# Two heads' probabilities transposed into one PSUM bank and copied by one ScalarE pass, in the first 48 heads of each layer

## Chip, cores and metric

The kernel runs on one core of a Trainium2 chip. The metric is the device time of one execution in microseconds, as the median of the runs. Engines are written PE (TensorE), DVE (VectorE), ACT (ScalarE), POOL (GpSimd) and SP (SyncE); QB, below, is the projection of the second head group's queries.

## What is computed

A decoder trunk of two layers over 512 positions and a width of 1024, in fp32. Each layer has a mixer with two groups of eight heads of 64 (group A: a sliding window of 128 with a sink for each head; group B: the 128 keys with the highest indexer score for each query), then a SwiGLU of width 2816. Cut to the part that the change touches:

```python
# group A, blocks of 128 queries against the previous and the own block of keys
s = einsum('bnqhgd,bnkhd->bnhgqk', qb, kk) * D ** -0.5      # masked to the band
p = softmax(concat([s, sink], -1), axis=-1)[..., :-1]
o = einsum('bnhgqk,bnkhd->bnqhgd', p, vv)
# group B, 128 queries against the selected keys (here: all keys up to the block, the others masked)
p = softmax(where(valid, s, -inf), axis=-1)
o = einsum('bqhgn,bqnhd->bqhgd', p, vs)
y = concat([rms_norm(ya, g_a), rms_norm(yb, g_b)], -1) @ w_o
```

## The kernel before

It is written engine by engine, in raw queues: each engine runs a fixed list of instructions in order, and semaphores (`wait_ge`) tie the lists together. Weights stream in as pieces of 128x1024; ACT rounds a piece to a high half, DVE (or POOL) subtracts it to get the low half, and PE forms each product from three matmuls (`split_product`, L631 to L633).

Attention of a layer is one software pipeline, `attention(l)`, which stands on PE (L1047), on ACT (L1398) and on DVE (L1926) with the same step counter i. It goes over 64 heads n = 8u + h: eight units u of eight heads. Units 0 to 3 are group A, tiles 0 to 3 of 128 queries; units 4 to 7 are group B, tiles 0, 1, 3, 2. A head has as many key blocks of 128 as `keys_of` says: 1 in unit 0, 2 in units 1 to 3, 1 in unit 4, 2 in unit 5, 4 in unit 6, 3 in unit 7. So the first 48 heads have at most 256 keys.

In step i, in this order:

- PE: scores of head i (`head_scores`, L941; from head 48 on two heads at a time every second step, `pair_scores`), transposes of the probabilities of head i-3 (`transpose_p`, L962), in the steps of `QB_STEPS` (1, 4, 6, 9, 11, 14, 16, 19, 21, 24, 26, 29, 31) a projection step of six matmuls of 512 columns (`project_qb`), values of head i-5 (`head_values`, L974), in steps 9, 21, 30 and 45 the transposes of roped queries (`transpose_q`), and every eighth step the transposes of a finished y (`transpose_y`).
- ACT: the copy of the transposed probabilities of head i-3 from PSUM to `pT` (`copy_p`, L1365; in units 6 and 7 heads 3 and 7 are copied by DVE instead, L1743), the exponential of head i (`exponential`, L1357), after some steps the evacuation of a projection, the square, scaling and high half of a finished y, a copy of transposed queries, and in steps 42, 47, 52 and 57 a weight conversion.
- DVE: rounds of the top-128 search (`top_max`, `top_replace`), the mask of head i (`mask_scores`, L1719), which writes `prob`, and the normalisation and low half of a finished y.

Scores lie in banks 3 and 4 in turn (three banks from head 40 on), so the score of head n waits for the mask of head n-2. The transposed probabilities lie in bank 6 or 7 by the parity of the head, so the transposes of head n wait for the copy of head n-2 (`wait_pT`, L380). `prob` and `pT` are rings of four slots of 512 columns; the mask of head n waits for the transposes of head n-4, the copy of head n for the values of head n-4. With L970 the page means the transposes, with L992 the value products, with L959 and L938 the scores, with L1371 ACT's copy, with L1362 its exponential, with L1739 the mask.

Of the kernel before, what the change touches and what calls it, by code (L numbers as in the profile page):

```python
# [11 lines left out]
ACT = mybir.ActivationFunctionType  # L12
# [53 lines left out]
PAIRS_FROM = 48  # L66
PT_RING = 4
# [49 lines left out]
def build_trunk(nc, x, c_col, positions, inv_freq, weights, w_ada, b_ada, b_gate, ln_col, ln_row, sinks, g_col, out):  # L117
    with ExitStack() as ctx:
# [260 lines left out]

        def wait_pT(eng, l, u, h):  # L380

            flat = [(a, b) for a in range(8) for b in range(HEADS) if (a, b) <= (u, h)]
            n_dve = sum(on_dve(a, b) for a, b in flat)
            if on_dve(u, h):
                eng.wait_ge(pT_dve, l * dve_heads + n_dve)
            else:
                eng.wait_ge(pT_act, l * (64 - dve_heads) + len(flat) - n_dve)
# [234 lines left out]
        def _(pe):  # L622
# [339 lines left out]
            def transpose_p(l, u, h):  # L962
                lo, hi = keys_of(UNITS[u])
                pe.wait_ge(probs, at_head(l, u, h))
                if before := back(u, h, 2):

                    wait_pT(pe, l, *before)
                n = 8 * u + h
                for b in range((hi - lo) // P):
                    m = pe.transpose(bank[6 + h % 2][:, b * P:(b + 1) * P],  # L970
                                     prob[:, n % P_RING, b * P:(b + 1) * P], ident[:])
                m.then_inc(p_transposed, 1)

            def head_values(l, u, h):  # L974
# [16 lines left out]
                for b in range(nb):  # L991
                    m = pe.matmul(bank[u % 2][:, h * HD:h * HD + w], pT[:, h % PT_RING, b * P:(b + 1) * P],  # L992
# [54 lines left out]
            def attention(l):  # L1047
                in_bank2 = ("chunk", 3)
                for i in range(64 + LAG_Y):
# [4 lines left out]
                    if 0 <= i - LAG_T < 64:  # L1054
                        transpose_p(l, (i - LAG_T) // 8, (i - LAG_T) % 8)
# [211 lines left out]
        def _(act):  # L1267
# [89 lines left out]
            def exponential(l, u, h):  # L1357
# [3 lines left out]
                p = prob[:, n % P_RING, 0:hi - lo]  # L1361
# [3 lines left out]
            def copy_p(l, u, h):  # L1365
                lo, hi = keys_of(UNITS[u])
                act.wait_ge(p_transposed, at_head(l, u, h))
                if before := back(u, h, PT_RING):

                    act.wait_ge(av_done, at_head(l, *before))  # L1370
                nc.scalar.activation(pT[:, h % PT_RING, 0:hi - lo], bank[6 + h % 2][:, 0:hi - lo], ACT.Copy)\  # L1371
# [26 lines left out]
            def attention(l):  # L1398
                for i in range(64 + LAG_SPLIT):
                    if 0 <= i - LAG_T < 64:  # L1400
                        u, h = (i - LAG_T) // 8, (i - LAG_T) % 8
                        if not on_dve(u, h):
# [122 lines left out]
        def _(dve):  # L1525
# [193 lines left out]
            def mask_scores(l, u, h):  # L1719
# [6 lines left out]
                if n >= P_RING:  # L1726
                    dve.wait_ge(p_transposed, at_head(l, u, h) - P_RING)
# [11 lines left out]
                nc.vector.tensor_tensor_reduce(out=prob[:, n % P_RING, 0:hi - lo], in0=s_bank(n)[:, 0:hi - lo],  # L1739
# [460 lines left out]
```

## Time and profile before

| | |
|---|---|
| median of 3 runs | 1275.48 us (1275.37 to 1276.41) |
| the profiled execution | 1276.25 us, of which the span is 1274.6 us |
| granted clock of TensorE | 0.998 of full speed |
| busy: PE, DVE, ACT, POOL | 1235.8, 801.5, 510.5, 274.2 us |
| attention loops | about 128 to 236 us (layer 0) and 751 to 855 us (layer 1) |

The profile is one execution of the program. Its tables give busy time by engine, groups of instructions by source line and shape, with the idle time of the engine just ahead of them and what ended that idle time (the releaser), and timelines: one row for each instruction or run of equal instructions, by its start in us from the start of the span. A matmul row's duration reaches beyond the start of the next one, because matmuls are pipelined; the distance between starts is their pitch. The same holds in part for ACT and DVE. PE is busy nearly all the time, so what is read in the timelines is where it is not, and how far ahead of its reader each ACT or DVE result comes.

### The profile page before, as it was taken

What the parts mean: (1) busy time and instruction counts of PE and PEld (TensorE: products, weight loads), DVE (VectorE), ACT (ScalarE), POOL (GpSimd) and SP (SyncE); (2) the same over time, 40 slices, a digit from 0 to 9 for tenths busy, and PEclk for the clock granted to TensorE, in tenths of its full rate; (3) what the DMA queues carried; (4) which work ended last, traced back from release to release, by engine and by line L of the source; (5) the groups of instructions that cost most, each with busy time, mean ns of one, the idle gap of its engine ahead of it and who ended that gap; (6) DMA issues with size and microseconds to landing.
All of it is one profiled execution on the core that took longest, in us unless ns stands there. A gap on an engine that the chain in (4) does not pass through costs nothing. (4 is left out here: it accounts for less than half of the span.)

```text
span 1274.6 us, 18347 instructions
## 1 busy us (share of the span) xinstructions
PE 1235.8 (97%) x6394; PEld 1031.6 (81%) x6394; DVE 801.5 (63%) x1400; ACT 510.5 (40%) x1027; POOL 274.2 (22%) x281
## 2 busy tenths in 40 slices
PE   6999989999999999999999999999999999999997
PEld 5778876889888888888888688778988888888886
DVE  6889997677777764333676699856733355433338
ACT  3555568345232212222145466862643321222220
POOL 4027236600111010000007367570000000000000
PEclk9999999999999999999999999999999999999999
DMA  9672012334878554222523120112232223332211
GB/s 358 240 270 79 33 51 67 132 116 150 279 264 270 193 168 175 90 93 98 171 94 117 66 67 2 37 63 84 75 124 99 97 101 132 99 98 89 94 65 66
DMA packets 44850, 158.30 MB, mean 124 GB/s; under 512 B 5872, under 2 KB 5872, under 8 KB 44784
## 3 DMA queue, kind: packets, MB, share of 16 engines
q1 hardware_dynamic: 30528, 109.07, 24.8%
q0 software_dynamic: 12960, 47.19, 10.9%
q10 hardware_dynamic: 1296, 1.17, 0.3%
q8 instruction: 40, 0.66, 0.2%
q14 instruction: 26, 0.21, 0.1%
HBM read 155.31 MB, written 2.10 MB: 123 GB/s over the span
## 5 line engine op out<-in xcount | busy, mean ns | idle before, releaser
L631 PE MATMUL bank<-hT_hi,w_hi 128*128 128x512 f32 x640 | 249.5, 390 | 0.0
L633 PE MATMUL bank<-hT_hi,w_lo 128*128 128x512 f32 x640 | 249.0, 389 | 0.0
L632 PE MATMUL bank<-hT_lo,w_hi 128*128 128x512 f32 x640 | 249.0, 389 | 0.0
L1967 DVE TENSOR_TENSOR w_lo<-w_raw,w_hi 128x1024 fp32r<-128x1024 f32 x88 | 107.9, 1226 | 147.0 <-ACT w_hi L1434 147.0
L1280 ACT ACTIVATE w_hi<-w_raw 128x1024 fp32r<-128x1024 f32 x96 | 100.7, 1062 | 202.8 <-PE bank L633 189.0
L1434 ACT ACTIVATE w_hi<-w_raw 128x1024 fp32r<-128x1024 f32 x88 | 93.0, 1057 | 161.1 <-PE bank L633 155.8
L631 PE MATMUL bank<-w_hi,hT_hi 128*128 128x512 f32 (+2 forms) x392 | 148.1, 378 | 2.9 <-ACT pq L1316 2.0
L1544 DVE TENSOR_TENSOR w_lo<-w_raw,w_hi 128x1024 fp32r<-128x1024 f32 x88 | 114.1, 1310 | 53.6 <-ACT w_hi L1280 52.2
L633 PE MATMUL bank<-w_hi,hT_lo 128*128 128x512 f32 (+2 forms) x392 | 142.6, 364 | 0.0
L632 PE MATMUL bank<-w_lo,hT_hi 128*128 128x512 f32 (+2 forms) x392 | 142.3, 363 | 0.0
L633 PEld LDWEIGHTS bank<-hT_hi,w_lo 128*128 128x128 f32 x640 | 120.1, 188 | 25.3
L631 PEld LDWEIGHTS bank<-hT_hi,w_hi 128*128 128x128 f32 x640 | 120.1, 188 | 24.8
L632 PEld LDWEIGHTS bank<-hT_lo,w_hi 128*128 128x128 f32 x640 | 120.1, 188 | 24.6
L631 PE MATMUL bank<-w_hi,gu_hi 128*128 128x512 f32 x264 | 102.9, 390 | 0.0
L633 PE MATMUL bank<-w_hi,gu_lo 128*128 128x512 f32 x264 | 102.7, 389 | 0.0
L632 PE MATMUL bank<-w_lo,gu_hi 128*128 128x512 f32 x264 | 102.7, 389 | 0.0
L478 POOL TENSOR_TENSOR rs_out<-rs_in,minus_half 128x1 f32<-128x1 f32 x31 | 21.4, 690 | 349.8 <-DVE rs_in L1814 325.3
L1993 DVE TENSOR_TENSOR gu<-bank,silu_g 128x512 f32<-128x512 f32 x44 | 30.4, 692 | 102.2 <-PE bank L633 101.8
L631 PEld LDWEIGHTS bank<-w_hi,hT_hi 128*128 128x128 f32 x392 | 73.9, 188 | 21.6 <-issue 7.0
L1427 ACT ACTIVATE silu_g<-bank 128x512 f32<-128x512 f32 x44 | 26.3, 598 | 156.2 <-PE bank L633 149.7
L633 PEld LDWEIGHTS bank<-w_hi,hT_lo 128*128 128x128 f32 x392 | 73.8, 188 | 11.6
L632 PEld LDWEIGHTS bank<-w_lo,hT_hi 128*128 128x128 f32 x392 | 74.0, 189 | 9.9 <-issue 0.5
(207 smaller groups left out, 2199.5 us busy)
## 6 DMA issues: line engine op xcount, KB each, us to landing
w_raw<-in_weights SPq DMA_DIRECT2D x184, 512.0 KB, 3.5
ada_w<-in_w_ada POOLq DMA_DIRECT2D x80, 512.0 KB, 5.2
ada_w<-in_w_ada SPq DMA_DIRECT2D x4, 512.0 KB, 6.6
qT<-in_w_ada SPq DMA_DIRECT2D x4, 512.0 KB, 10.0
xs<-in_x SPq DMA_DIRECT2D x4, 512.0 KB, 15.4
g_row<-in_ln_row POOLq DMA_DIRECT2D x4, 512.0 KB, 5.2
b_row<-in_ln_row POOLq DMA_DIRECT2D x4, 512.0 KB, 6.1
trunk_out<-xs SPq DMA_DIRECT2D x8, 256.0 KB, 2.1
```

The lines of the kernel that those rows point to most:

```text
L478: nc.gpsimd.tensor_tensor(rs_out[:, n:n + 1], rs_in[:, n:n + 1], minus_half[:], ALU.pow)\
L631: pe.matmul(dst, a_hi, b_hi, start=first, stop=False)
L632: pe.matmul(dst, a_hi, b_lo, start=False, stop=False)
L633: return pe.matmul(dst, a_lo, b_hi, start=False, stop=last)
L1280: nc.scalar.activation(w_hi[:, p % RING, :], w_raw[:, p % RING, :], ACT.Copy).then_inc(hi_ready, 1)
L1427: nc.scalar.activation(silu_g[:, f, :], bank[GU_BANK[g] + 2 * f][:], ACT.Silu)\
L1434: nc.scalar.activation(w_hi[:, s, :], w_raw[:, s, :], ACT.Copy).then_inc(hi_ready, 1)
L1544: nc.vector.tensor_tensor(w_lo[:, p % RING, :], w_raw[:, p % RING, :], w_hi[:, p % RING, :].bitcast(F32), ALU.subtract).then_inc(lo_ready, 1)
L1967: nc.vector.tensor_tensor(w_lo[:, s, :], w_raw[:, s, :], w_hi[:, s, :].bitcast(F32), ALU.subtract).then_inc(lo_ready, 1)
L1993: nc.vector.tensor_tensor(gu[:, f, :], bank[GU_BANK[g] + 2 * f + 1][:], silu_g[:, f, :], ALU.mult).then_inc(gu_ready, 1)
```

## The change

For heads n below `NARROW` = 48, the heads are handled in pairs (n even, n+1). PE does the transposes of both in the step in which it did those of the odd one (step n+4), into one bank: the even head's blocks in the first half of the used columns, the odd one's behind; pairs alternate between banks 6 and 7. ACT copies the pair by one pass of up to 512 columns into one slot of `pT`, at the place where it copied the odd head; the copy of the even head is gone. `prob` holds eight heads, two in a slot of 512 columns, and the mask of head n waits for the transposes of head n-8. The value products read their half of the slot and wait for the pair's copy. The copy waits for the values of eight heads before (the slot's last user). From head 48 on the code is as before, with its semaphore counts adjusted.

```diff
--- before.py
+++ after.py
@@ -64,6 +64,7 @@
 
 QB_FREE = 40
 PAIRS_FROM = 48
+NARROW = 48
 PT_RING = 4
 DVE_HEADS = (3, 7)
 
@@ -377,14 +378,29 @@
 
         dve_heads = 2 * len(DVE_HEADS)
 
+        def prob_of(n, w):
+
+            if n < NARROW:
+                return prob[:, n % 8 // 2, n % 2 * 256:n % 2 * 256 + w]
+            return prob[:, n % P_RING, 0:w]
+
+        def pT_of(n, w):
+
+            if n < NARROW:
+                return pT[:, n // 2 % PT_RING, n % 2 * w:(n % 2 + 1) * w]
+            return pT[:, n % PT_RING, 0:w]
+
         def wait_pT(eng, l, u, h):
 
-            flat = [(a, b) for a in range(8) for b in range(HEADS) if (a, b) <= (u, h)]
-            n_dve = sum(on_dve(a, b) for a, b in flat)
+            n = 8 * u + h
+            n_dve = sum(on_dve(m // HEADS, m % HEADS) for m in range(n + 1))
+            by_act = NARROW // 2 + 64 - NARROW - dve_heads
             if on_dve(u, h):
                 eng.wait_ge(pT_dve, l * dve_heads + n_dve)
+            elif n < NARROW:
+                eng.wait_ge(pT_act, l * by_act + n // 2 + 1)
             else:
-                eng.wait_ge(pT_act, l * (64 - dve_heads) + len(flat) - n_dve)
+                eng.wait_ge(pT_act, l * by_act + n + 1 - NARROW // 2 - n_dve)
 
         def back(u, h, n):
 
@@ -961,14 +977,19 @@
 
             def transpose_p(l, u, h):
                 lo, hi = keys_of(UNITS[u])
+                n = 8 * u + h
+                w = hi - lo
                 pe.wait_ge(probs, at_head(l, u, h))
-                if before := back(u, h, 2):
+                if before := back(u, h, 2 if n >= NARROW else 3 + h % 2):
 
                     wait_pT(pe, l, *before)
-                n = 8 * u + h
-                for b in range((hi - lo) // P):
-                    m = pe.transpose(bank[6 + h % 2][:, b * P:(b + 1) * P],
-                                     prob[:, n % P_RING, b * P:(b + 1) * P], ident[:])
+                if n < NARROW:
+                    b0, at = 6 + n // 2 % 2, n % 2 * w
+                else:
+                    b0, at = 6 + h % 2, 0
+                for b in range(w // P):
+                    m = pe.transpose(bank[b0][:, at + b * P:at + (b + 1) * P],
+                                     prob_of(n, w)[:, b * P:(b + 1) * P], ident[:])
                 m.then_inc(p_transposed, 1)
 
             def head_values(l, u, h):
@@ -989,7 +1010,8 @@
 
                 w = P if h < HEADS - 1 else HD
                 for b in range(nb):
-                    m = pe.matmul(bank[u % 2][:, h * HD:h * HD + w], pT[:, h % PT_RING, b * P:(b + 1) * P],
+                    m = pe.matmul(bank[u % 2][:, h * HD:h * HD + w],
+                                  pT_of(8 * u + h, hi - lo)[:, b * P:(b + 1) * P],
                                   v[:, lo // P + b, g:g + w], start=b == 0, stop=b == nb - 1)
                 m.then_inc(av_done, 1)
 
@@ -1051,7 +1073,10 @@
                         head_scores(l, i // 8, i % 8)
                     elif i < 64 and i % 2 == 0:
                         pair_scores(l, i // 8, i % 8)
-                    if 0 <= i - LAG_T < 64:
+                    if 0 <= i - LAG_T < NARROW and (i - LAG_T) % 2 == 1:
+                        transpose_p(l, (i - LAG_T - 1) // 8, (i - LAG_T - 1) % 8)
+                        transpose_p(l, (i - LAG_T) // 8, (i - LAG_T) % 8)
+                    elif NARROW <= i - LAG_T < 64:
                         transpose_p(l, (i - LAG_T) // 8, (i - LAG_T) % 8)
                     if i in QB_STEPS:
                         project_qb(l, QB_STEPS.index(i) // CP[4], QB_STEPS.index(i) % CP[4])
@@ -1358,16 +1383,21 @@
                 lo, hi = keys_of(UNITS[u])
                 n = 8 * u + h
                 act.wait_ge(masked, at_head(l, u, h))
-                p = prob[:, n % P_RING, 0:hi - lo]
+                p = prob_of(n, hi - lo)
                 nc.scalar.activation(p, p, ACT.Exp, scale=-1.0, bias=nmax[:, u % 2, h:h + 1],
                                      accum_out=rowsum[:, u % 2, h:h + 1]).then_inc(probs, 1)
 
             def copy_p(l, u, h):
                 lo, hi = keys_of(UNITS[u])
+                n = 8 * u + h
                 act.wait_ge(p_transposed, at_head(l, u, h))
-                if before := back(u, h, PT_RING):
+                if before := back(u, h, 8 if n < NARROW else PT_RING):
 
                     act.wait_ge(av_done, at_head(l, *before))
+                if n < NARROW:
+                    nc.scalar.activation(pT[:, n // 2 % PT_RING, 0:2 * (hi - lo)],
+                                         bank[6 + n // 2 % 2][:, 0:2 * (hi - lo)], ACT.Copy).then_inc(pT_act, 1)
+                    return
                 nc.scalar.activation(pT[:, h % PT_RING, 0:hi - lo], bank[6 + h % 2][:, 0:hi - lo], ACT.Copy)\
                     .then_inc(pT_act, 1)
 
@@ -1399,7 +1429,7 @@
                 for i in range(64 + LAG_SPLIT):
                     if 0 <= i - LAG_T < 64:
                         u, h = (i - LAG_T) // 8, (i - LAG_T) % 8
-                        if not on_dve(u, h):
+                        if not on_dve(u, h) and (i - LAG_T >= NARROW or h % 2 == 1):
                             copy_p(l, u, h)
                     if i < 64:
                         exponential(l, i // 8, i % 8)
@@ -1723,8 +1753,9 @@
                 n = 8 * u + h
                 dve.wait_ge(scored, at_head(l, u, h))
 
-                if n >= P_RING:
-                    dve.wait_ge(p_transposed, at_head(l, u, h) - P_RING)
+                ring = 2 * P_RING if n < NARROW else P_RING
+                if n >= ring:
+                    dve.wait_ge(p_transposed, at_head(l, u, h) - ring)
                 else:
                     dve.wait_ge(qk_transposed, at_chunk(l, 2, T - 1))
                 if h == 0 and u >= 2:
@@ -1736,7 +1767,7 @@
                 else:
                     mask = scores[:, SC_AT[t]:SC_AT[t] + hi - lo] if t > 0 else band[:, P:2 * P]
                     start = 3.0e38
-                nc.vector.tensor_tensor_reduce(out=prob[:, n % P_RING, 0:hi - lo], in0=s_bank(n)[:, 0:hi - lo],
+                nc.vector.tensor_tensor_reduce(out=prob_of(n, hi - lo), in0=s_bank(n)[:, 0:hi - lo],
                                                in1=mask, scale=-(HD ** -0.5), scalar=start, op0=ALU.add,
                                                op1=ALU.min, accum_out=nmax[:, u % 2, h:h + 1]).then_inc(masked, 1)
```

## Rows read from the trace of the kernel before

**Rows 1.** The page, part 1: busy us, share of the span, instructions.

```profile
PE 1235.8 (97%) x6394; PEld 1031.6 (81%) x6394; DVE 801.5 (63%) x1400; ACT 510.5 (40%) x1027; POOL 274.2 (22%) x281
```

**Rows 2.** Windows of the attention loops: us, busy us (x instructions) by engine, clock, DMA.

```profile
core 0: us, PE busy (x) PEld busy (x) DVE busy (x) ACT busy (x) POOL busy (x), PEclk, DMA share, GB/s
...
140.00:183.00 43.00, 41.40 (x255) 35.10 (x254) 41.85 (x132) 26.85 (x86) 11.37 (x12) 1.00 0.11 38
183.00:200.00 17.00, 12.82 (x90) 10.71 (x91) 12.55 (x53) 13.30 (x49) 11.36 (x10) 1.00 0.20 63
200.00:212.00 12.00, 11.80 (x84) 8.73 (x82) 9.30 (x32) 10.73 (x31) 9.25 (x7) 1.00 0.27 89
212.00:240.00 28.00, 26.85 (x192) 21.80 (x193) 16.91 (x43) 19.50 (x47) 21.84 (x15) 1.00 0.13 39
750.00:860.00 110.00, 103.96 (x687) 86.47 (x686) 85.97 (x294) 77.30 (x238) 75.51 (x59) 1.00 0.10 34
```

**Rows 3.** Groups by shape: count, busy us, mean ns, idle before and its releaser.

```profile
L970 PE MATMUL bank<-ident,pq 128*128 128x128 f32 x272 | 51.8, 277 | 6.2 <-ACT pT L1371 5.1 <-DVE pT L1749 1.1
...
L1371 ACT ACTIVATE pT<-bank 128x256 f32<-128x256 f32 x64 | 23.9, 373 | 5.1 <-PE bank L970 5.1
...
L1371 ACT ACTIVATE pT<-bank 128x512 f32<-128x512 f32 x12 | 7.0, 585 | 0.0
```

**Rows 4.** Timeline of PE, layer 0: start, us, instruction [idle before <-releaser].

```profile
164.12 0.61 PE L992 MATMUL bank<-v_a,pT 128*128 128x128 f32 x4
165.13 0.70 PE L959 MATMUL bank<-kT,qT 128*128 128x256 f32 x2 [0.40 <-DVE nmax L1739]
166.01 0.41 PE L970 MATMUL bank<-ident,pq 128*128 128x128 f32 x2 [0.18 <-ACT pT L1371]
166.89 0.50 PE L631 MATMUL bank<-w_hi,hT_hi 128*128 128x512 f32 x1 [0.47 <-ACT pq L1316]
...
181.79 0.38 PE L970 MATMUL bank<-ident,pq 128*128 128x128 f32 x2
...
183.47 0.38 PE L970 MATMUL bank<-ident,pq 128*128 128x128 f32 x2
183.69 0.61 PE L992 MATMUL bank<-v_a,pT 128*128 128x128 f32 x4
...
185.27 0.41 PE L970 MATMUL bank<-ident,pq 128*128 128x128 f32 x2 [0.75 <-ACT pT L1371]
```

**Rows 5.** Timeline of ACT, layer 0, copies of heads 19 and 29.

```profile
165.49 0.38 ACT L1371 ACTIVATE pT<-bank 128x256 f32<-128x256 f32 x1
...
184.76 0.36 ACT L1371 ACTIVATE pT<-bank 128x256 f32<-128x256 f32 x1
```

**Rows 6.** Timeline of PE, layer 0: q transposes, values of heads 42 and 44.

```profile
199.76 0.63 PE L898 MATMUL bank<-ident,pq 128*128 128x128 f32 x4 [0.84 <-DVE hT_lo L1789]
...
201.97 0.61 PE L992 MATMUL bank<-v_b,pT 128*128 128x128 f32 x4
...
204.58 0.61 PE L992 MATMUL bank<-v_b,pT 128*128 128x128 f32 x4
```

**Rows 7.** Timeline of ACT, layer 0: copy 43, exponential 46, copy 45.

```profile
202.34 0.37 ACT L1371 ACTIVATE pT<-bank 128x256 f32<-128x256 f32 x1
202.60 0.51 ACT L1362 ACTIVATE pq<-pq,nmax 128x256 f32<-128x256 f32 x1
...
205.41 0.38 ACT L1371 ACTIVATE pT<-bank 128x256 f32<-128x256 f32 x1
```

**Rows 8.** Timeline of PE, layer 1: values 18, a projection step, values 28.

```profile
786.02 0.61 PE L992 MATMUL bank<-v_a,pT 128*128 128x128 f32 x4
...
787.77 0.50 PE L631 MATMUL bank<-w_hi,hT_hi 128*128 128x512 f32 x1 [0.47 <-ACT pq L1316]
...
803.77 0.61 PE L992 MATMUL bank<-v_a,pT 128*128 128x128 f32 x4
```

**Rows 9.** Timeline of ACT, layer 1, copies of heads 19 and 29.

```profile
786.37 0.37 ACT L1371 ACTIVATE pT<-bank 128x256 f32<-128x256 f32 x1
...
803.63 0.36 ACT L1371 ACTIVATE pT<-bank 128x256 f32<-128x256 f32 x1
```

## The prediction, made before the changed kernel ran

> **What bounds the kernel now.** I read the busy times of the page first, then the table by stretch, the groups by shape, and last the timelines of TensorE (PE) and ScalarE (ACT), step by step. PE is busy 97% of the span [rows 1], so only its idle time can be won or lost. No matmul or transpose is added or removed; the forecast is therefore a sum of PE waits inside the two attention loops. In layer 0's loop PE idles 1.6 of 43 us while VectorE (DVE) is 97% busy (140 to 183 us), then 4.2 of 17, 0.2 of 12 and 1.15 of 28 us; ACT is busy 62%, 78% and 89% of the first three stretches. Layer 1 idles 6.0 of 110 us [rows 2]. After the loop PE has no idle time worth the name until the next stage, so a microsecond that PE loses in the loop is lost at the end.
>
> **How a head's copy stands to its readers.** Call T(n) the transposes of head n, C(n) its copy, A(n) its value product. PE does T(n) in step n+3 and A(n) in step n+5; ACT does C(n) in step n+3, behind the exponential of head n+2. The change makes T(n), T(n+1) of an even head and their one copy all happen in step n+4. Three things follow for A(n), n even:
> - By the end of T(n+1) PE has done the same work as before, so that moment stays. A(n) comes one T earlier, because T(n+2) is no longer in between: a T of two blocks has a pitch of 0.22 us (183.47 to 183.69) [rows 4].
> - The pair's copy can start no earlier than C(n+1) does today, since ACT still does the exponential of n+3 first. It takes 0.59 us instead of 0.37, by the form of 512 columns [rows 3]. I use 0.60, plus 0.04 for the hand-over to PE.
> - So A(n) is late by (start of C(n+1) + 0.64) - (start of A(n) - 0.22). Today A(n) needs only C(n), which is one ACT step older.
>
> Where a projection step (six 512-column matmuls) or a y transpose lies between T(n+1) and A(n), the wait is hidden by it: so it is, step by step in the timelines, for heads 0 to 6, 14, 16 and 20 to 26. Without that cover, A(n) follows T(n+1) by only 0.88 us (one A and one score), and ACT, which does two exponentials, a root's scaling or a 1 us conversion in front, is later than that.
>
> **The sum, layer 0.** Waits don't add up: a PE that has waited once comes later to the next place, so each place counts against the shift that is there already, and today's waits behind it vanish.
> - Head 18: C(19) starts at 165.49, A(18) at 164.12 [rows 5, 4]: 166.13 - 163.90 = 2.2 us late. Behind it three waits vanish (0.40, 0.18, 0.47) [rows 4]: 1.2 us stay. Heads 8, 10 and 12 are late too, by less; they lie ahead of it and are contained in it.
> - Head 28: C(29) at 184.76, A(28) at 183.69: 185.40 - 183.47 = 1.9 late [rows 4, 5]; the 0.75 wait at 185.27 vanishes [rows 4]: 1.2. But C(29) is itself behind DVE, which is full until 183 and which the first shift of 1.2 sets back (a full queue that is started later ends later), by an estimated 0.2. I take 1.4 us; ends 0.7 (DVE catches up) and 1.9 (the 0.75 isn't recovered).
> - Heads 34 to 40: late as well, but at 199.76 PE waits 0.84 for DVE's low half of y [rows 6], which hangs on ACT; ACT gets there no later with one copy fewer. Nothing is added: that wait is the cover. Were it gone, this would cost another 0.8.
> - Head 42: C(43) starts at 202.34 [rows 7]; its ACT step then holds one copy fewer, so about 202.1, done 202.7; A(42) would come at 201.9 [rows 6]: 0.8 late. Head 44: C(45) at 205.41, behind a scaling and a conversion, about 205.2 in the new order, so A(44) at 205.8 in place of 204.58 [rows 6, 7]; with T(46) (0.22) still to be done and matmul tails of 0.1 taken off, 1.4 us. No QB step, y transpose or DVE wait stands there. Ends 0.8 (ACT gains more) and 1.7 (A(44) waits for the full ACT order of today).
> - Heads 48 to 63 keep their code. All idle time there is 1.15 us [rows 2], part of it waits on DVE that move with PE. I give back 0.35; ends 0 and 1.15.
>
> Layer 0: 1.4 + 0 + 1.4 - 0.35 = 2.45 us.
>
> **Layer 1.** Head 18: C(19) at 786.37, A(18) at 786.02 [rows 8, 9]: 787.01 - 785.80 = 1.2 late, less the 0.47 wait at 787.77 [rows 8]: 0.7. Head 28: C(29) at 803.63, A(28) at 803.77: 804.27 - 803.55 = 0.7 late [rows 8, 9] against unshifted queues; DVE is nearly full here too and mostly moves with the shift, so I add about two thirds: 1.2; ends 0.7 and 1.5. The rest is the same pattern to 0.1 us. 1.2 + 1.4 - 0.35 = 2.25 us.
>
> **What comes free.** 24 ACT copies a layer fall away, but the next ACT instruction starts 0.26 us after a copy of 256 columns (202.34 to 202.60) [rows 7] and, by my estimate from the duration of the 512 form, about 0.48 after one of 512: 0.04 a pair, 1.9 us in all of ACT, off PE's path except where used above. PE's waits for a free transpose bank (5.1 us in all, heads behind 48 included) [rows 3] vanish in the first 48 heads; the sum has them, since each was set against the wait that takes its place. Probabilities in eight slots in place of four: DVE masks head n behind its score, and T(n-4) stands ahead of that score in PE's queue today, so that wait is never the last and lifting it is worth 0; eight slots are needed only because T of an even head now comes behind the score of head n+4. At the border, T(48) waits for the copy of heads 46 and 47: PE first does one A and the y transposes, 0.44 us each by the pitch of such groups, and the copy needs 0.64: 0 to 0.5, taken 0. No DMA is moved; POOL's root and gain work follows ACT's conversions and moves with them.
>
> ACT is not saturated outside 200 to 212 us, and its lateness is what PE waits for [rows 2]. The Trainium skill (Perfetto Trace Analysis, Optimizing Scalar/DVE Operations) says that grouping into larger operations helps if the engine is saturated, and that where Scalar or Vector are not saturated but cause bubbles elsewhere, breaking instructions up may let work finish sooner. By the first sentence the change would win, by the second lose; this trace's 62% and 78% stand on the second's side. By the first alone the sum would be a gain of the 1.9 us of ACT, 1273.6 us; by the second it is the sum below.
>
> **Sum.** 2.45 + 2.25 = 4.7 us. The profiled execution took 1276.25 us (span 1274.6 and 1.65 around it), so 1280.95 for it; that execution is 0.77 above the median of the three runs (1275.48), so **1280.2 us** for the median.
>
> **Rivals.**
> - *The early shift is absorbed.* ACT and DVE have enough lead that heads 18 and 28 cost nothing net, and only heads 42 to 44 do: 2 x 1.05 = 2.1 us, 1277.6 us. For it: DVE, not PE, limits 140 to 183 [rows 2], and PE waited for it at 165.13 [rows 4]. Against: A(28) lies behind that, and its own copy is late. Chance 0.21.
> - *Faster: the bank waits were the limit.* One mechanism: PE's waits for a transpose bank vanish (up to 5.1 us) [rows 3] and A(n) finds its copy done, because ACT's order has room. It decides if the pair's copy ends within 0.88 us of T(n+1), that is, if ACT idles when T(n+1) ends. Price -3 to -5: about 1271.6 us. For it: those waits are real [rows 4]. Against: ACT doesn't idle there: C(29) starts 2.6 us behind the end of T(29) (181.79 + 0.38 to 184.76) [rows 4, 5]. Chance 0.08.
> - *The waits add up.* The shift is passed on by DVE and ACT to every later copy, so that the late heads, thirteen a layer, all count. The six priced above run from 0.7 to 2.2 us; at an estimated 1 us each they make 26, less the bank waits 21. Half of that is about 11 us: 1287 us. Against: the cover at 199.76 [rows 6]. Chance 0.08.
> - The forecast itself: 0.63.
>
> **Chances.** A measurement of this kernel tells about 0.2% (2.6 us) from no change. Slower by more: 0.63 less a tenth for its low end, plus 0.08, plus a quarter of the first rival: 0.70. Within: 0.20. Faster: 0.10. The ends of the terms give +2.0 to +7 us (1277.5 to 1282.5); the range reaches down through the first rival, 1276.0, and up halfway to the third, 1284.5.
>
> **What would show it.** Right: PE idle ahead of the value products (L992's line) that is absent now, at heads 10, 12, 18, 28, 34, 36 and 40 to 44, ended by ACT's copy; copies of 512 columns at 0.59 us; idle ahead of the transposes nearly gone in the first 48 heads; PE busy unchanged. A(44) of layer 0 about 2.8 us later than 204.58. Wrong: copies that start within 0.2 us of T(n+1); new waits at the score products or in DVE that are longer than the old ones; a shift at 200 us of zero.

## The result, and the profile after

The changed kernel takes 1280.87 us (median of 6 runs, 1279.41 to 1282.21), the kernel before on the same chip 1275.57 us (6 runs, 1275.29 to 1276.41): ratio 1.0039, 95% interval 1.0029 to 1.0050. It is 5.3 us slower. The direction and the size of the forecast (1280.2 us) hold; several of its steps don't, and some errors cancel.

Two executions of the changed kernel were profiled. The first took 1282.21 us (span 1280.5) and is called *after*. The second took 1280.06 us (span 1278.4) and is called *after, second trace*. They differ mainly in one thing, told under the hardware below: in the first, TensorE (PE) ran two stretches at half its clock. The accounts below use the second, which sets 1278.4 beside the 1274.6 of before: 3.8 us more.

The page of after answers to [rows 1]: busy us, share of the span, instructions.

```profile
PE 1238.7 (97%) x6394; PEld 1034.5 (81%) x6394; DVE 801.0 (63%) x1400; ACT 508.2 (40%) x979; POOL 273.7 (21%) x281
```

48 ScalarE (ACT) instructions are gone (1027 to 979) and with them 2.3 us of ACT; no PE instruction was added. In the second trace PE is busy for 1236.6 us, 0.8 more than before, so what the kernel lost is idle time of PE.

The same stretches as [rows 2], of the second trace of after.

```profile
core 0: us, PE busy (x) PEld busy (x) DVE busy (x) ACT busy (x) POOL busy (x), PEclk, DMA share, GB/s
140.00:183.00 43.00, 40.53 (x256) 34.96 (x255) 41.98 (x135) 25.45 (x75) 11.68 (x12) 1.00 0.11 38
183.00:200.00 17.00, 12.59 (x89) 10.68 (x90) 12.17 (x52) 13.55 (x43) 11.02 (x10) 1.00 0.18 63
200.00:212.00 12.00, 10.84 (x70) 7.41 (x69) 7.55 (x27) 10.41 (x27) 9.26 (x7) 1.00 0.28 89
212.00:240.00 28.00, 26.94 (x200) 22.07 (x200) 17.00 (x46) 19.49 (x48) 21.83 (x15) 1.00 0.12 39
750.00:860.00 110.00, 102.84 (x679) 85.35 (x677) 85.74 (x296) 76.80 (x215) 74.24 (x59) 1.00 0.09 30
```

Against [rows 2], PE's idle time grew by 0.9, 0.2 and 1.0 us in the first three stretches and by 1.1 us in layer 1's; it is the same to 0.1 us behind head 48.

The wide copy answers to the copies of [rows 3] (group by shape, after: busy, mean ns, idle before).

```profile
L1398 ACT ACTIVATE pT<-bank 128x512 f32<-128x512 f32 x32 | 18.7, 586 | 4.9 <-PE bank L991 4.9
```

And this is where the time went. PE's own waits in layer 0's loop (128 to 245 us), first before, then the second trace of after: engine, line waited at, what for; us in total, times, longest. L970 and L991 are the transposes, L992 and L1013 the value products, L959 and L975 scores, L898 and L914 the q transposes, each before and after.

```profile
PE bank L970 <- ACT pT L1371: 3.0, 6, 0.8
PE bank L959 <- DVE nmax L1739: 2.5, 5, 0.7
PE bank L631 <- ACT pq L1316: 1.0, 2, 0.6
PE bank L898 <- DVE hT_lo L1789: 0.8, 1, 0.8
```

```profile
PE bank L1013 <- ACT pT L1398: 7.5, 8, 1.8
PE bank L975 <- DVE nmax L1770: 1.2, 3, 0.8
PE bank L991 <- ACT pT L1401: 0.6, 1, 0.6
PE bank L647 <- ACT pq L1341: 0.4, 1, 0.4
```

Waits for a free bank (3.0 us) vanish in the first 48 heads, and so do most waits on VectorE (DVE); one new wait, of the value product for its pair's copy, takes 7.5 us in 8 places. With the small ones that aren't shown (0.8 us before, 0.5 after) the waits go from 8.1 to 10.2 us, 2.1 us more.

How the loss builds up can be read from the start of each value product against its start before. From the two traces (layer, head:shift in us; second trace of after):

```
layer 0  1:-0.3  9:0.0  13:0.6  19:0.0  27:0.0  29:0.8  39:0.8  41:0.2  43:0.9  45:1.8  47:1.9  51:1.5  63:1.5
layer 1  1:1.5   9:1.8  13:2.1  19:2.0  27:2.0  29:2.8  39:3.1  41:2.5  43:3.2  45:4.1  47:4.2  51:3.8  63:3.8
```

Layer 0's loop costs 1.8 us (-0.3 to 1.5), nothing is lost between the loops, layer 1's costs 2.3 (1.5 to 3.8). 4.1 us in all, less the 0.3 ahead of the first loop: the 3.8 of the spans. That 0.3 isn't the change: ahead of the first loop the code is the same, and traces with no half clock there reach head 1 up to 0.8 us earlier than before's (the kernel of experiment 3: 0.8). So the loops are read against their own start.

### The profile page after: what moved, and what is told of

It reads as the page before. It is cut to its first block and busy times, and to the rows that moved or that the text cites. A ratio compares the mean times of both kernels' runs of the same rounds, so it can differ in the third digit from the quotient of the medians.

```text
span 1280.5 us, 18247 instructions
## 1 busy us (share of the span) xinstructions
PE 1238.7 (97%) x6394; PEld 1034.5 (81%) x6394; DVE 801.0 (63%) x1400; ACT 508.2 (40%) x979; POOL 273.7 (21%) x281
## 5 line engine op out<-in xcount | busy, mean ns | idle before, releaser
L1387 ACT ACTIVATE pq<-pq,nmax 128x256 f32<-128x256 f32 (+3 forms) x128 | 66.3, 518 | 48.0 <-DVE nmax L1770 47.0
## 6 DMA issues: line engine op xcount, KB each, us to landing
qT<-in_w_ada SPq DMA_DIRECT2D x4, 512.0 KB, 10.2
```

Of the source, the lines that this page charges most:

```text
L1387: nc.scalar.activation(p, p, ACT.Exp, scale=-1.0, bias=nmax[:, u % 2, h:h + 1], accum_out=rowsum[:, u % 2, h:h + 1]).then_inc(probs, 1)
```

## The experiments

All medians stand beside the kernel before in the same session, at 1275.56 to 1275.68 us. Where a trace was at half clock somewhere in a loop, it is said.

**1. Value products a step later.** The wait is for a copy, so give the copy a step more.

```
-LAG_T, LAG_V = 3, 5
+LAG_T, LAG_V = 3, 6
```

> The changed kernel with the value product of head n in step n+6 in place of n+5. Theory (the pair's copy comes too late for the even head's value product, because it starts behind the exponential of head n+3): the value product gets one step (0.9 us) more, so most waits ahead of it vanish, and the bank waits ahead of the transposes (3.9 us in the first 48 heads of before) are gone too: 1272 to 1276 us, by my estimate 1274. Rival A (the loss is ACT's or DVE's throughput, or a slower clock, not the distance of copy and value product): stays at 1279 to 1281. Rival B (y is finished one step later and the normalisation, which stands in DVE's queue, now waits for it): 1278 or above with new waits of DVE on the value products.

Measured: 1278.37 us (1277.64 to 1279.21, 10 runs), ratio 1.0019 (1.0010 to 1.0029). The direction was right and the size missed. PE's four largest waits in 128 to 245 us:

```profile
PE bank L975 <- DVE nmax L1770: 3.1, 6, 0.8
PE bank L914 <- DVE hT_lo L1820: 1.7, 1, 1.7
PE bank L1013 <- ACT pT L1398: 1.5, 3, 0.7
PE bank L647 <- ACT pq L1341: 1.3, 2, 0.8
```

The wait for the pair's copy falls from 7.5 to 1.5 us; 2.5 us of the 5.3 come back. Rival B's time (1278 or above) came out too: here and in the trace of experiment 2, but not in before, DVE waits 1.6 us in two places ahead of the normalisation (the profile names its reciprocal, the instruction before, as what it waited for). So the rest had to be split into what the later step costs in itself and what pairing costs, which experiment 2 does.

**2. The kernel before with the same step**, the control of experiment 1 (the same line, in the kernel before).

> The kernel before with the value products of each head one step later (six steps behind its scores, not five); the control to the same edit of the changed kernel, which ran at 1278.4 us. Theory, third form (pairing costs because the even head's transposes and copy come a step closer to its value product; with a step more it has only its own small price left, and the end of each loop is later by one value product, 0.67 us a layer by the traces): 1276.9 us (1276.3 to 1277.8) here, and so 1.5 us (0.6 to 2.1) for pairing beside 5.3 us without the step. Rival (a later value product helps any kernel alike, since waits of other kinds are covered by it too): 1273 to 1275.5 us, and pairing costs 3 us or more with the step too.

Measured: 1277.14 us (1276.51 to 1278.54, 11 runs), ratio 1.0011 (1.0002 to 1.0020). As the theory had it. In its trace the transposes keep their times through the loops (head 9 to 63: 0.0 in layer 0, +0.2 in layer 1), and the last value product comes 0.67 us later against the last transposes in each: one product more behind the end of the loop. So with a step more, pairing costs 1278.37 - 1277.14 = 1.2 us; without it 5.3. The traces, none with half clock in a loop, say the same: by the starts of the transposes and of the last value product, the two loops cost 2.7 us in experiment 1 and 1.5 here, so pairing costs 1.2 with the step and 4.1 without it. So the step that it takes from the even head is about three quarters of its cost. The later step itself costs 1.6 us (1277.14 - 1275.58).

**3. Pairs in the first 32 heads alone.**

```
-NARROW = 48
+NARROW = 32
```

> The changed kernel with pairs in heads 0 to 31 only. Theory: heads 0 to 31 leave a shift of 1.3 us a layer (heads 18 and 28), which is carried on, less 0.3 later; heads 34 to 46 add another 1 us a layer in the full change and nothing here: 1275.6 + 2 = 1277.6 us (1277.0 to 1278.5). If the late part alone cost (first rival of the prediction turned round): 1275.6. If the early part is all of it: 1280 to 1281.

Measured: 1276.77 us (1276.49 to 1279.31, 11 runs), ratio 1.0010 (1.0001 to 1.0019), just below the expected range. PE's two largest waits of 128 to 188 us; the same two lines stand, word for word, in the second trace of after:

```profile
PE bank L1013 <- ACT pT L1398: 4.0, 3, 1.8
PE bank L975 <- DVE nmax L1770: 1.0, 2, 0.8
```

The same 4.0 us of waits for the copy stand here in the first 32 heads, and the kernel loses 1.1 us (1276.77 - 1275.68), not 5.3. By the starts of the value products the shift at head 31 is 1.05 us in layer 0 and 1.3 in layer 1, of which 0.8 and 0.5 are given back at heads 33 and 34, where heads are single again and their transposes a step earlier. So the 8 pairs from head 32 on carry the larger part of the loss: they lose time of their own, and with them nothing is given back.

**4. The exponential behind the copy.** The forecast said that ACT does the exponential of head n+3 in front of the pair's copy.

```
-                    if i < 64:
-                        exponential(l, i // 8, i % 8)
...
+                    late = i < NARROW + 3 and i % 2 == 1
+                    for n in range(i - 1 if i % 2 == 0 and 0 < i < NARROW + 3 else i, i if late else i + 1):
+                        if n < 64:
+                            exponential(l, n // 8, n % 8)
...
```

> The changed kernel with ACT's order altered: the exponential of each odd head stands behind the pair's copy of the next step, not ahead of it. Theory: the copy now starts right behind its transposes unless a conversion or a scaling is in front, ends 0.64 us later, and the value product comes 0.88 us behind the transposes; the waits at heads 10, 12, 18, 34 and 36 vanish and those at 28, 40 to 44 shrink by about 0.5 us: 1274 to 1277 us, 1275.5 taken. Rival (the length of the 512-column pass is what costs, not its place): stays within 0.5 us of the changed kernel's 1280.9. Rival (exponentials that come later hold up the transposes): above 1281.

Measured: 1280.97 us (1279.71 to 1283.54, 5 runs), ratio 1.0049 (1.0036 to 1.0063). The theory in this form falls. ACT at head 10 of layer 0 in this trace, which reaches the loop 0.8 us earlier than before's (start, us, instruction, idle before):

```profile
147.68 0.60 ACT L1411 ACTIVATE bank<-pk 128x512 f32<-128x512 f32 x1 [1.59 <-DVE pk L1805]
...
148.31 0.58 ACT L1398 ACTIVATE pT<-bank 128x512 f32<-128x512 f32 x1
```

and in after (the first trace, 0.3 us later than before's at the loop's start):

```profile
147.74 0.51 ACT L1387 ACTIVATE pq<-pq,nmax 128x256 f32<-128x256 f32 x1 [1.04 <-DVE nmax L1770]
...
148.78 0.60 ACT L1411 ACTIVATE bank<-pk 128x512 f32<-128x512 f32 x1 [0.44 <-DVE pk L1803]
...
149.41 0.58 ACT L1398 ACTIVATE pT<-bank 128x512 f32<-128x512 f32 x1
```

The exponential was moved, and the square of y, which waits for DVE's normalisation, still stands in front of the copy. Against the start of its loop the copy comes at the same time as before the move: 1.1 us earlier in absolute time, and the loop began 1.1 us earlier; in both traces it starts 2.05 us behind its pair's last transposes (146.26 to 148.31, 147.36 to 149.41). At other heads the move did act. At head 18 the copy stands 1.3 us behind its transposes and not 2.0, and the shift at head 31 is 0.3 us against the loop's start, where the second trace of after has 1.1. But at head 34 ACT idles 2.18 us for the same normalisation with nothing left to do, the copy stands 2.6 us behind its transposes in place of 1.5, and at the end layer 0 has lost 2.0 us, where the second trace of after has 1.8.

**5. One pass made two, in the same place.**

```
...
-                    nc.scalar.activation(pT[:, n // 2 % PT_RING, 0:2 * (hi - lo)],
-                                         bank[6 + n // 2 % 2][:, 0:2 * (hi - lo)], ACT.Copy).then_inc(pT_act, 1)
+                    for w in (slice(0, hi - lo), slice(hi - lo, 2 * (hi - lo))):
+                        nc.scalar.activation(pT[:, n // 2 % PT_RING, w], bank[6 + n // 2 % 2][:, w], ACT.Copy)\
+                            .then_inc(pT_act, 1)
```

> The changed kernel with the pair's single pass split into two passes of one head each, at the same place, both behind the second head's transposes; the value product of the even head waits for the first alone. Theory: the first copy ends 0.22 us sooner, so each place where the wait is the last loses 0.2: head 28 and heads 42 and 44 (which add) give 0.5 to 0.6 us a layer back: 1279.6 to 1280. So grouping itself costs about 1 us in all, and moving the even head's transposes and copy a step back costs the other 4. Rival (the wide pass is the cost): 1276 to 1277. Rival (fewer ACT instructions are a gain that holds the loss down): above 1281.

Measured: 1280.69 us (1278.52 to 1282.25, 5 runs), ratio 1.0039 (1.0026 to 1.0053). The copies are narrow again (duration min/median/max ns):

```profile
L1397 ACT ACTIVATE pT<-bank x96: 255/368/400, 133.1 to 830.6; 128x256 f32<-128x256 f32 x64, 128x128 f32<-128x128 f32 x32
```

and the kernel is as slow as with one pass: 0.2 us less, inside the spread, and above the 1279.6 to 1280 that were expected. The rival (the wide pass is the cost) falls. The pass itself costs next to nothing: layer 0 loses 1.5 us here and 1.8 in the second trace of after, so at most 0.3 us a layer (layer 1's trace had a stretch of half clock and doesn't compare).

**6. All side jobs of y a step later**, and three of the copies of q and one conversion as well; and the kernel before with the y jobs moved. ACT's side jobs (square, scaling and splitting of y, and most of the q copies and conversions) fall on the odd steps, directly ahead of a pair's copy. The first edit is made in the changed kernel and in the kernel before; the second comes on top of it in the changed kernel:

```
-LAG_NORM, LAG_ROOT, LAG_SCALE, LAG_Y, LAG_SPLIT = 6, 7, 8, 11, 12
+LAG_NORM, LAG_ROOT, LAG_SCALE, LAG_Y, LAG_SPLIT = 6, 8, 9, 12, 13
...
-                    for lag, part in ((LAG_NORM, square_y), (LAG_SCALE, scale_y), (LAG_SPLIT, split_y)):
+                    for lag, part in ((LAG_NORM + 1, square_y), (LAG_SCALE, scale_y), (LAG_SPLIT, split_y)):
```

```
-QB_AT = (9, 21, 30, 45)
+QB_AT = (10, 22, 30, 46)
...
-WO_AT = (42, 47, 52, 57)
+WO_AT = (42, 48, 52, 57)
```

> The changed kernel with ACT's square, scaling and high half of a finished y (and what hangs on them on DVE, POOL and PE) one step later. Today they stand in ACT's queue at the end of odd steps, directly ahead of the pair's copy; one step later they stand behind it. Theory (second form: the copy is late for what ACT's odd step holds, and the exponential is the smaller part of that): the waits at heads 10, 12, 28, 34, 36 and 40 go to below 0.3 us each; those at 18, 42 and 44 keep a q copy or a conversion in front and stay at about half: 1275.5 to 1278 us, 1276.8 taken. Rival (pairing itself makes PE wait, wherever the jobs stand): 1280 to 1281. Rival (a y that is ready one step later delays the end of the loop or DVE): 1278 to 1281 with new waits at the y transposes or the masks.

> As e5_y_jobs_behind, and also the q copies of steps 9, 21 and 45 and the conversion of step 47 one step later, so that no extra ACT job stands at an odd step before head 48 is reached. Theory: the last large waits, at heads 18, 42 and 44, go too, and what is left is the exponential of head n+3 in front: 1274 to 1276.5 us, 1275.3 taken, 1 us or more below e5. Rival (as e5: pairing itself): 1280 to 1281. Rival (ACT's even steps are overfull, since copy, exponential and job now meet there): at or above e5.

> The kernel before with the same shift of the y jobs by one step, no pairs: the control for e5. Theory: in the kernel before each head has a copy of its own in each step, so parity is of no account; some bank waits move, 1275 to 1276.5 us. If this kernel gets slower than before by as much as e5 stays above it, what is left in e5 is the y that comes later and not pairing; if it gets faster, e5's gain is in part not of pairing.

Measured: 1288.79 us with the y jobs moved (4 runs, ratio 1.0099, 1.0082 to 1.0116), 1289.33 us with all of them (4 runs, 1.0105, 1.0088 to 1.0122) and, for the kernel before with the y jobs moved, 1287.88 us (4 runs, 1.0095, 1.0078 to 1.0112). All missed: the move itself costs 12.3 us without pairs and 7.9 with them. All three traces have stretches of half clock in or at the end of the loops (that of the kernel before four, of 3.4 us each), so some of this is the clock. PE's two largest waits and ACT's largest in the kernel before with the move, 195 to 245 us:

```profile
PE bank L992 <- ACT pT L1371: 2.5, 1, 2.5
PE bank L898 <- DVE hT_lo L1789: 1.6, 1, 1.6
```

```profile
ACT pk L1388 <- POOL rs_out L478: 3.9, 3, 2.7
```

ACT now waits up to 2.7 us for POOL's root at the scaling, and PE once 2.5 us for a copy, which stands behind that in ACT's order. Both are at the end of the loop (ACT's scaling starts at 236.74, PE's product at 237.89), behind the narrow heads. On this ground pairing costs 0.9 us (1288.79 - 1287.88), but the ground has so many waits of its own that this says little of the kernel as it is.

**7. The side jobs behind the copy on ACT alone.** A cleaner form: no lag is changed; ACT does the side jobs of an odd step behind the copy that opens the next.

```
+                    if 0 < i <= 50 and i % 2 == 0:
+                        extras(i - 1)
                     if i < 64:
                         exponential(l, i // 8, i % 8)
...
+                    if i > 50 or i % 2 == 0:
+                        extras(i)
```

Here extras(i) is the square, scaling, splitting, q copy and conversion of step i as they were. It ran with 48 paired heads, in the kernel before, and with 32 paired heads.

> The changed kernel, with ScalarE's side jobs of each odd step (square, scaling and splitting of y, copy of q, weight conversion) moved behind the pair's copy that opens the next step, and ahead of that step's exponential; nothing else is moved, on no other engine. Theory, second form (what stands between the odd step and the pair's copy in ScalarE's own order makes the copy late, 2.2 to 2.4 us a layer): the waits ahead of the even heads' value products at 10, 12, 28, 34, 36, 40, 42 and 44 shrink to 0.5 us or less and the time is 1275.5 us (1274.5 to 1277.0). Rival (two heads in one pass are late whatever stands ahead of them): 1280 to 1281 us. Second rival (a side job done even half a step later holds up the transposes of y, as moving it by a whole step did): above 1282 us, and then the kernel before with the same edit is above 1277 us too.

> The kernel before with the same move of ScalarE's side jobs from each odd step to behind the copy that opens the next. Theory: nothing waits for them there, 1275.6 us (1275.0 to 1276.2). Second rival: above 1277 us.

> As the changed kernel with the side jobs behind the copy, with pairs in the first 32 heads alone. Theory: late copies are gone and so little is left for the number of pairs to change: 1275.6 us (1275.0 to 1276.5), within 0.5 us of the same edit with 48 heads. Rival (pairs cost whatever stands ahead of them): 1276.8 us as without the move, and 4 us less than with 48 heads.

Measured: 1282.93 us (1281.32 to 1283.89, 5 runs), ratio 1.0052 (1.0038 to 1.0066); the kernel before 1279.22 us (1278.60 to 1280.08, 8 runs), ratio 1.0026 (1.0016 to 1.0037); 32 paired heads 1281.39 us (1281.00 to 1281.64, 5 runs), ratio 1.0044 (1.0031 to 1.0058). The second rival's numbers came out: the move costs the kernel before 3.6 us by itself, and pairing costs 3.7 us on top of it. The theory's time (1275.5) missed, and so did its word on 32 heads (1.5 us less than with 48, not within 0.5) and the rival's (4 us less). PE's two largest waits with 48 paired heads, 128 to 245 us:

```profile
PE bank L975 <- DVE nmax L1776: 3.3, 4, 1.0
PE bank L1013 <- ACT pT L1398: 3.2, 6, 0.9
```

The wait for the pair's copy falls from 7.5 to 3.2 us: the side jobs did stand in its way. Waits of the scores for DVE are 3.3 us, where the second trace of after has 1.2. Which of the jobs moved costs the kernel before its 3.6 us was not tried. And head 44 shows what no reordering on ACT removes (ACT, then PE):

```profile
206.94 0.60 ACT L1398 ACTIVATE pT<-bank 128x512 f32<-128x512 f32 x1 [0.92 <-PE bank L991]
```

```profile
206.24 0.66 PE L991 MATMUL bank<-ident,pq 128*128 128x128 f32 x4
206.74 0.61 PE L1013 MATMUL bank<-v_b,pT 128*128 128x128 f32 x4
207.59 0.71 PE L1013 MATMUL bank<-v_b,pT 128*128 128x128 f32 x4 [0.24 <-ACT pT L1398]
```

ACT was idle and started the copy the moment the pair was transposed, and PE still waited: only one value product lies between the transposes and the product that needs them. The traces with 48 and with 32 paired heads had one stretch of half clock each in layer 0's loop (185.1 to 188.5 and 200.2 to 203.6 us), the one of the kernel before had none, so the 3.7 and 2.2 us (1281.39 - 1279.22) of the medians can hold some of the clock. Layer 1's loop is at full clock in all three traces: against before it costs 4.1 us with 48 paired heads, 3.3 with 32 and 2.4 with none. So pairing adds 1.8 us there with 48 heads, where it costs 2.3 without the move. In that layer the side jobs in front of the copy account for about a fifth of the price, not for nearly all of it as the theory had it.

**8. The changed kernel again, profiled.**

> The changed kernel once more, for a second trace. If a drop of the granted clock to 1.2 GHz inside the first attention loop (3.4 us at 186 us in the first trace) is a regular part of the change, it is there again. If it is chance, it is absent, the span is about 1 us shorter, and the shift that each layer leaves is 2.0 to 2.6 us all the same.

Measured: 1280.06 us, one run, the second trace used above. The drop of the clock is absent, so it is no regular part of the change; the span is 2.1 us shorter (about 1 was expected), and the layers leave 1.8 and 2.3 us (2.0 to 2.6 were expected).

None of these kernels is faster than the kernel before.

## Why the prediction was right, point by point

**The bound and the mechanism: right.** PE's idle time is what moved, DVE and ACT were not the bound, and the new wait is of the value product for the pair's copy. The places named were heads 10, 12, 18, 28, 34, 36 and 40 to 44; in the second trace a value product starts 0.05 us (0.05 being the hand-over from ACT to PE) behind the end of its pair's copy at heads 8, 10, 12, 18, 28, 32, 34, 36, 40, 42 and 44 of layer 0 (8 and 32 weren't named; PE idles 0.03 and 0.12 us ahead of them). Experiments 1 and 2 confirm it: with a step more for the copy, pairing costs 1.2 us and not 5.3. The transposes' waits for a free bank fell from 3.0 to 0.6 us in layer 0's loop, as forecast, and the 0.6 lie behind head 48; no transpose waits for a pair's copy in the second trace, so the border at head 48 was worth the 0 it was taken at.

**The copy's duration: right.** 586 ns, where 0.59 was taken.

**What stands in front of the copy: in part.** The text named the exponential of head n+3, a root's scaling and a conversion. The square of y and DVE's normalisation ahead of it, which hold the copy at heads 10 and 34, aren't named; taking the exponential away (experiment 4) or the side jobs (7) gives back little or nothing. What the runs show is the distance: the even head's product has one step less.

**Head 18: half right.** PE there, second trace of after:

```profile
165.60 0.71 PE L1013 MATMUL bank<-v_a,pT 128*128 128x128 f32 x4 [1.80 <-ACT pT L1398]
166.15 0.60 PE L975 MATMUL bank<-kT,qT 128*128 128x256 f32 x2
166.58 0.60 PE L991 MATMUL bank<-ident,pq 128*128 128x128 f32 x4
166.94 0.47 PE L647 MATMUL bank<-w_hi,hT_hi 128*128 128x512 f32 x1
```

Against 164.12 in [rows 4] the product starts 1.48 later, and 1.8 us relative to the trace's start of the loop (-0.3), where 2.2 was forecast; ACT's copy started at 164.96, not 165.49, with copies fewer in front. But 1.2 us were to stay, and the projection step behind it starts at 166.94 where it started at 166.89 [rows 4]: 0.35 us stay. The waits that vanish were mis-sized. I summed the idle column (0.40, 0.18, 0.47: 1.05). From the product's start to the projection's it was 2.77 us before and is 1.34 now, 1.43 less, and two more transposes lie in it now. Read from start to start, a wait is larger than its idle column: a score is followed by its successor 0.43 us after its own start (166.15 to 166.58), though its record is 0.60 long, and the idle column counts only from the record's end. Before, that pitch was 0.88 us (165.13 to 166.01) with 0.18 in the idle column [rows 4]: 0.45 us lost, 0.18 listed.

**Head 28: right in kind, too large.** Second trace, PE and ACT:

```profile
185.07 0.71 PE L1013 MATMUL bank<-v_a,pT 128*128 128x128 f32 x4 [1.76 <-ACT pT L1398]
```

```profile
183.81 0.72 ACT L1418 ACTIVATE pk<-pk,rs_out 128x512 f32<-128x512 f32 x1 [0.31 <-POOL rs_out L494]
184.44 0.58 ACT L1398 ACTIVATE pT<-bank 128x512 f32<-128x512 f32 x1
```

The forecast set this copy back by 0.2 us because a full DVE would be set back. It started at 184.44, 0.32 us *earlier* than 184.76 [rows 5], which is just the 0.3 by which this loop began earlier: with only 0.3 us of shift arriving from PE, none was passed on. The shift after head 28 is 1.1 us against the loop's start (0.8 and 0.3), where 1.4 was summed.

**The cover at 199.76: the step that failed.** I had "nothing is added" for heads 34 to 40 and kept the 1.4 us through it. PE, second trace, from the value product of head 40:

```profile
199.18 0.71 PE L1013 MATMUL bank<-v_b,pT 128*128 128x128 f32 x4 [0.72 <-ACT pT L1398]
199.73 0.60 PE L914 MATMUL bank<-ident,pq 128*128 128x128 f32 x4
...
202.67 0.71 PE L1013 MATMUL bank<-v_b,pT 128*128 128x128 f32 x4 [0.59 <-ACT pT L1398]
...
206.04 0.71 PE L1013 MATMUL bank<-v_b,pT 128*128 128x128 f32 x4 [0.56 <-ACT pT L1398]
```

The q transposes start at 199.73, at 199.76 before [rows 6], and the wait of 0.84 us for DVE is gone. A wait for an engine that keeps its times absorbs the shift that arrives at it; of 1.1 us, 0.3 is left. ACT and DVE did keep theirs: DVE starts that low half at 198.68, at 198.92 before, which is 0.06 us later against the loop's start. My text said itself that a shift of zero at 200 us would be wrong for it: here it was -0.03 in absolute time, 0.3 against the loop's start. In layer 1 the same wait [0.85 us] vanished, and the shift went from 1.6 to 0.8 us against the loop's start.

**Heads 42 and 44: right as times, wrong as a sum.** Unshifted, A(44) was forecast for 205.8; it came at 206.04. The text then put 1.4 us of early shift on top ("about 2.8 us later than 204.58", 207.4). ACT kept its times: copy 45 starts at 205.41 in both kernels [rows 7] (the text had 205.2 for it). Second trace of after, ACT:

```profile
203.83 0.72 ACT L1418 ACTIVATE pk<-pk,rs_out 128x512 f32<-128x512 f32 x1 [0.24 <-POOL rs_out L494]
204.46 1.05 ACT L1305 ACTIVATE w_hi<-w_raw 128x1024 fp32r<-128x1024 f32 x1
205.41 0.57 ACT L1398 ACTIVATE pT<-bank 128x512 f32<-128x512 f32 x1
```

So these heads lose up to their own lateness whatever came before: 1.8 us (0.3 to 2.1 against the loop's start), not 1.4. What I wrote of waits at the head of the sum, that each counts against the shift that is there already, holds here too, and I didn't apply it.

**Behind head 48:** -0.3 us in layer 0 and in layer 1, -0.35 forecast.

**The sum.** Layer 0: 1.1 - 0.8 + 1.8 - 0.3 = 1.8 us, forecast 1.4 + 0 + 1.4 - 0.35 = 2.45. Layer 1: 1.6 - 0.8 + 1.8 - 0.3 = 2.3, forecast 2.25, which hit because an absorption not counted (0.8) stood against an early part (1.6 for 1.2; 0.3 of it grew at heads 32 to 38, where nothing was to be added) and late heads (1.8 for 1.4) that were too small. That it hit is luck. 4.1 us in the loops, forecast 4.7. The profiled executions differ by 3.8 us, the medians by 5.3. The rest is that before's profiled execution lies 0.7 us above its median, and the second trace's 0.8 below that of the changed kernel. The clock (below), which no term had, may be the cause of the latter; that isn't shown.

**The rivals.** *The early shift is absorbed* was half right: its outcome at 200 us is what the trace shows, though by the wait at the q transposes and not by a lead of ACT; its time (1277.6) fails because heads 42 to 44 then cost 1.8 us and not 1.05. Experiment 3 prices the early heads: pairs in the first 32 alone cost 1.1 us. *Faster* fails as its own condition said: the copy starts 2.0 us behind the pair's last transposes at head 18, far from at once (0.6 us in layer 1). *The waits add up* fails; 11 late places in layer 0 hold 7.6 us of idle time (8 of them the 7.5 us above) and cost 1.8.

**The rule on grouping.** ACT was spared 2.3 us of work and the kernel got 5.3 us slower: of the two sentences of the Trainium skill (Perfetto Trace Analysis, Optimizing Scalar/DVE Operations) weighed in the prediction, the trace speaks against the first, and the second fits in its condition (ACT isn't saturated and PE waits for it) but not in its remedy: broken up into two narrow passes in the same place (experiment 5), the first copy has to wait for the second head's transposes all the same and the kernel is as slow. What counts is when the first half becomes available.

## What to carry to other kernels

Joining two producers into one pass delays the first one's reader to the second one's time, plus whatever stands ahead in the copying engine's queue; before doing it, count the work between the second producer and the first reader, and lengthen that distance by a step (here that cut the price from 5.3 to 1.2 us, and cost 1.6 us itself, so the kernel stayed slower than the one that doesn't join). Price a wait from start to start, not by its idle column. When shifts are summed along an engine, stop at each place where it waits for an engine that keeps its own times: there the sum starts anew, downwards and upwards.

## What was not expected of the hardware

**The granted clock fell inside the loops, in some executions.** Windows of after, first trace (PEclk is the granted clock, 1.00 for 2.4 GHz, 0.50 for 1.2), then the middle one in the second trace:

```profile
184.00:186.00 2.00, 0.34 (x3) 0.34 (x4) 1.97 (x9) 1.70 (x7) 0.37 (x1) 1.00 0.69 215
186.20:189.40 3.20, 3.20 (x17) 3.20 (x16) 0.30 (x2) 1.64 (x6) 2.77 (x3) 0.50 0.02 8
189.60:192.00 2.40, 2.24 (x18) 1.85 (x16) 1.13 (x6) 1.25 (x4) 1.40 (x2) 1.00 0.03 7
```

```profile
186.20:189.40 3.20, 3.08 (x28) 2.89 (x27) 0.91 (x5) 2.29 (x8) 3.12 (x3) 1.00 0.02 5
```

PE had been idle for most of 2 us at head 28 (busy 0.34 of 2.00) and then ran 17 matmuls where the other execution ran 28. The stretch reached from 186.1 to 189.5 us and cost 1.6 us: the two traces of after agree in the shift of their value products up to head 27, to a constant of 0.6 us, and from head 31 on are 1.6 us further apart. The 0.6 is what a second stretch of half clock, at 32.5 to 35.9 us in the first trace, left: that trace was 0.9 us ahead of the second one up to it, and is 0.6 behind it afterwards, so that this stretch cost 1.5 us. The 1.6 and the 0.6 make 2.2 us, which is the difference of the two executions (1282.21 and 1280.06).

Such stretches stand inside the attention loops in seven of the thirteen traces of kernels other than before: the changed kernel's first, that of experiment 5, all three of experiment 6, and those with 48 and 32 paired heads of experiment 7. There is none in the loops of the kernel before, in experiments 1 to 4, in experiment 7's kernel before and in the second trace. That PE's new waits bring them is suggested by where they stand, and not shown; but a wait of 1.76 us at the same head was there in the second trace without one, so a wait alone doesn't decide it. What does was not tried and stays open. It could account for the changed kernel's wider spread (1279.41 to 1282.21 against 1275.29 to 1276.41) and for what the loops don't show of the 5.3 us.
